# A feed-forward made from the residual times the norm's weight, with the norm's inverse by token multiplied into gate and value

## What is computed

```python
def rms_norm_2(x, gain):
    xf = x.astype(jnp.float32)
    y = xf * lax.rsqrt(jnp.mean(xf * xf, axis=-1, keepdims=True) + EPS)
    return (y * gain.astype(jnp.float32)).astype(x.dtype)
...
        mix = jnp.concatenate([lru_o, gla_o], axis=-1) @ w_out[l]
        x = x + mix

        h = rms_norm_2(x, norm2[l])
        gate, up = jnp.split(h @ w_ffn_in[l], 2, axis=-1)
        x = x + (jax.nn.silu(gate) * up) @ w_ffn_out[l]
    return rms_norm_2(x, final_norm)
```

## Time and profile before

| | us |
|---|---|
| median of 3 timed runs | 2332.33 (2331.25 to 2334.07) |
| profiled execution, its time | 2328.58 |
| profiled execution, its span | 2327.3 |
| TensorE busy in the span | 2258.5 (97%) |
| VectorE busy | 1410.2 (61%) |
| ScalarE busy | 1045.0 (45%) |
| GpSimd busy | 985.5 (42%) |

### The profile page before, as it was taken

One profiled execution on the slowest core, in us unless ns is written; L12 is line 12 of the kernel. 1 busy time (PEld: TensorE's weight loads), 2 busy tenths in 40 slices (PEclk: granted clock), 3 DMA queues, 4 the chain that ended last, 5 costly groups with the idle time before them and its releaser, 6 DMA issues.

```text
span 2327.3 us, 29639 instructions
## 1 busy us (share of the span) xinstructions
PE 2258.5 (97%) x11342; PEld 1795.0 (77%) x11342; DVE 1410.2 (61%) x1784; ACT 1045.0 (45%) x1644; POOL 985.5 (42%) x674
## 2 busy tenths in 40 slices
PE   5999999999999999999999999999999999999998
PEld 5888755478888888866688677888878888888887
DVE  6256678668885275268845663442876666666665
ACT  5323265488883264357734562222333333333334
POOL 1111188546652138853122121122365555665551
PEclk9999999999999999999999999999999999999999
DMA  8255300010003133220031311132111111111111
GB/s 318 78 154 161 118 1 5 5 34 1 1 1 118 37 130 109 73 73 11 34 103 43 126 37 37 37 118 64 28 54 55 55 55 55 54 46 47 55 55 73
DMA packets 156385, 154.74 MB, mean 66 GB/s; under 512 B 12550, under 2 KB 141620, under 8 KB 154324
## 3 DMA queue, kind: packets, MB, share of 16 engines
q1 hardware_dynamic: 156244, 152.84, 21.1%
HBM read 128.05 MB, written 20.97 MB: 64 GB/s over the span
## 4 chain that ended last, share of the span: by engine, by line
PE 84%; ACT 5%; DVE 4%; issue 3%; POOL 2%; DMA 1%; SPq 0%; ACTq 0%; DVEq 0%; POOLq 0%
PE ps L256 29%; PE ps L3219 15%; PE ps L3236 9%; PE ps L1946 6%; PE ps L1366 3%; PE ps L1377 2%; PE ps L1165 2%; PE ps L2256 2%; PE ps L2239 2%; PE ps L2225 2%; PE ps L1188 2%; PE ps L1175 1%; PE ps L1348 1%; POOL WSL L3136 1%; ACT B_PR L1249 1%
## 5 line engine op out<-in xcount | busy, mean ns | idle before, releaser
L243 POOL TENSOR_TENSOR WL<-WR,WH 128x1024 fp32r<-128x1024 f32 (+2 forms) x71 | 163.9, 2309 | 656.2 <-ACT WH L238 656.0
L256 PE MATMUL ps<-HH,WH 128*128 128x512 f32 (+2 forms) x880 | 279.8, 399 | 0.4 <-issue 0.3
L256 PE MATMUL ps<-HL,WH 128*128 128x512 f32 (+2 forms) x880 | 273.6, 392 | 0.0
L256 PE MATMUL ps<-HH,WL 128*128 128x512 f32 x848 | 263.2, 392 | 0.0
L3449 DVE TENSOR_TENSOR XF<-ps,XF 128x1024 f32<-128x1024 f32 x168 | 201.6, 1220 | 32.5 <-PE ps L3236 25.9
L3219 PE MATMUL ps<-HC,WSH 128*128 128x512 f32 x640 | 197.1, 389 | 0.0
L256 PEld LDWEIGHTS ps<-HL,WH 128*128 128x128 f32 (+2 forms) x880 | 164.0, 186 | 37.7
L256 PEld LDWEIGHTS ps<-HH,WH 128*128 128x128 f32 (+2 forms) x880 | 160.2, 187 | 38.1 <-issue 5.3
L256 PEld LDWEIGHTS ps<-HH,WL 128*128 128x128 f32 x848 | 160.5, 189 | 34.2
L3136 POOL TENSOR_TENSOR WSL<-WSR,WSH 128x512 fp32r<-128x512 f32 x100 | 131.4, 1314 | 107.5 <-ACT WSH L3130 107.5
L3130 ACT ACTIVATE WSH<-WSR 128x512 fp32r<-128x512 f32 x100 | 62.9, 629 | 218.2 <-POOL WSR L3118 218.2
(11 more groups left out here) (460 smaller groups left out, 5309.6 us busy)
## 6 DMA issues: line engine op xcount, KB each, us to landing
WS<-in_w_ffn_in SPq DMA_DIRECT2D x44, 512.0 KB, 5.1
MKW<-in_ada_w SPq DMA_DIRECT2D x32, 512.0 KB, 4.1
spill<-X SPq DMA_DIRECT2D x3, 4096.0 KB, 13.9
OW<-in_w_ffn_out SPq DMA_DIRECT2D x22, 512.0 KB, 3.6
WR<-in_w_in SPq DMA_DIRECT2D x19, 512.0 KB, 3.8
WR<-in_even_w_in SPq DMA_DIRECT2D x17, 512.0 KB, 4.1
AWK<-in_ada_w SPq DMA_DIRECT2D x8, 1024.0 KB, 9.3
X<-spill SPq DMA_DIRECT2D x2, 4096.0 KB, 13.6
```

Source lines behind the costliest of these rows:

```text
L243: pool.tensor_tensor(low[:, :, :], raw[:, :, :], high[:, :, :].bitcast(F32), ALU.subtract).then_inc(*w_low.up(t))
L256: last = pe.matmul(ps[0:w.out, 2 * s + h, :], wt[:, k, :], x[:, k, halves(h)], start=(k == 0 and n == 0), stop=(k == w.kt - 1 and n == len ...
```

## The change

- The blocks are made from the residual times `norm2` alone, without the inverse by token. So they no longer wait for the norm: each follows its output tile on VectorE, its high part is made by ScalarE and its low part by VectorE. HC is laid out anew, by feature, so that a block may overwrite those parts of HM and LM that the last output tile has read.
- The token sums and the spread are made between the products of pair 0, whose order is by pairs of features (0, 4), (1, 5), (2, 6), (3, 7). The `pe_stay_awake` around them goes.
- ScalarE copies the spread inverse to TOKENS. Gate and value are multiplied by it: in pairs 0 and 1 as they leave PSUM (`dve_plain`, 1024 wide), in pairs 2 to 21 by four instructions of 512 on VectorE (`dve_by_token`). Silu then reads CG.
- TOKENS takes the place at 139.5 KB, where OWL was; OWL now lies on OW (131.5 KB). So OW(j) may be loaded only after y(j-1, 7), the last that reads the parts before it. The last pair has an OW of its own. SP asks for WS a pair earlier in its list.
- In pair 1 the tiles of y(0) stand otherwise between the products: 2, 3, 3 and none.

```diff
     def pe_second_out():
         for f, t in enumerate(S_OUT):
-            pe_tile(t, HM, LM, made=(lambda k: m_low.at(2, k)) if f == 0 else None)
-        pe_stay_awake(8, 4)
-        pe_token_sums(3, 4, LAST.sq)
-        pe_stay_awake(5, 5)
-        pe_spread(3, LAST)
-        pe_stay_awake(13, 0)
+            if f < DT - 1:
+                pe_tile(t, HM, LM, made=(lambda k: m_low.at(2, k)) if f == 0 else None)
+        for k in range(DT):
+            last = pe_feature(t, k, HM, LM)
+            if k % 2 and k < DT - 1:
+                last.then_inc(*out_freed.up("mix", k))
...
             dve_residual(t, f, at=LAST)
+            dve_block(f)
             dve_add_square(3, f, LAST.sq)
+        for k in BLOCKS[:4]:
+            dve_block_low(k)
         dve_last_residual(t, at=LAST)
+        dve_block(DT - 1)
+        for k in BLOCKS[4:6]:
+            dve_block_low(k)
         for h in range(2):
             dve_add_last_square(3, h, LAST.sq)
+        for k in BLOCKS[6:]:
+            dve_block_low(k)
...
-    OW = place("OW", 131.5, [P, DM])
+    OW = [place("OW0", 131.5, [P, DM]), place("OW1", 63, [P, DM])]
     A_OW = [[place(f"{n}{i}", kb, [P, SEQ], F32R) for n, kb in zip(("AH", "AL", "OWH", "OWL"), kbs)]
-            for i, kbs in enumerate(((115, 127.5, 135.5, 139.5), (51, 55, 59, 63)))]
+            for i, kbs in enumerate(((115, 127.5, 135.5, 131.5), (39, 47, 55, 63)))]
+    TOKENS = place("TOKENS", 139.5, [P, SEQ])
...
         for j in range(NPAIR):
             if j:
-                sp_pair(j)
+                if j + 1 < NPAIR:
+                    sp_pair(j + 1)
+                sp.wait_ge(*(y_done.at(j - 1, DT - 1) if j < NPAIR - 1 else ws_used.at(at_use(j, M5))))
                 sp.wait_ge(*ow_low.at(j - 1))
             else:
                 sp.wait_ge(*w_used.at(S_OUT[-1]))
-            sp.dma_start(OW[:, :], d["w_ffn_out_2"][0][rows(j), :]).then_inc(*ow_loaded.landed(j))
+            sp.dma_start(out_weight(j), d["w_ffn_out_2"][0][rows(j), :]).then_inc(*ow_loaded.landed(j))
+            if j == 0:
+                sp_pair(1)
...
         else:
             dve.wait_ge(*b_low.at("block", DT - 1))
-            if o != M3:
-                dve.wait_ge(*b_sum.at(M3, 1))
+            dve.wait_ge(*(spread_turned.at(3) if o == M3 else b_sum.at(M3, 1)))
...
         if o == M5:
             dve_add(j, "3+5", M5, CG[:, N2], CG[:, N2], bank[BANK[M5]], copied=(M5, 0))
+            dve_by_token(j, CG, "gate", 1, "3+5")
...
             dve_add(j, "value", M1, CU[:, N2], CU[:, N2], bank[BANK[M1]], waits=("3-2+6",))
+            dve_by_token(j, CU, "value", 0, "2+4")
+            dve_by_token(j, CU, "value", 1, "value")
             dve_product(j, 1)
         elif o == M7:
             dve_add(j, "gate", M7, CG[:, N1], CG[:, N1], bank[BANK[M7]], waits=("1+4-5",))
+            dve_by_token(j, CG, "gate", 0, "gate")
             dve_a_low(j, 1)
             dve_product(j, 0)
             dve_a_low(j, 0)
 
+    def dve_by_token(j, values, name, h, made):
+
+        dve.wait_ge(*m_added.at(j, made))
+        dve.tensor_tensor(values[:, halves(h)], values[:, halves(h)], TOKENS[:, halves(h)], ALU.mult).then_inc(
+            *m_added.up(j, "scaled " + name, h))
+
+    def dve_plain(j, g, name, values):
+
+        if g == 0 and j == 0:
+            dve.wait_ge(*scale_copied.at("tokens"))
+        elif g == 0:
+            dve.wait_ge(*product_made.at(j - 1, 1))
+        dve.wait_ge(*ws_used.at(at_use(j, 2 * g + 1)))
+        dve.tensor_tensor(values[:, :], pair(2 * g), TOKENS[:, :], ALU.mult).then_inc(*m_added.up(j, name))
```

More of the change, by code:

```diff
@@ L2999, in more @@
                     act_weight_high(0, o)
+                for k in BLOCKS[:-1]:
+                    act_block_high(k)
         act_out_tiles(S_OUT, 3, more, at=LAST)
+        act_block_high(BLOCKS[-1])
         act_root(3)
@@ L3190, in pe_plain @@
             pe.wait_ge(*b_low.at("block", k))
-        elif k == 0:
-            pe.wait_ge(*(product_made.at(j - 1, 1) if g else silu_made.at(j - 1)))
+        if k == 0:
+            pe.wait_ge(*(m_added.at(j - 1, "value" if g else "gate") if j else ev_dve.at(S_OUT[DT - 2:][(S_OUT[0] + g) % 2])))
         for m, (w, x) in enumerate(((WSH, 0), (WSH, 1), (WSL, 0))):
             for n in range(2):
-                last = pe.matmul(ps[:, 2 * g + n, :], w[:, q % RING, i, :], HC[c][:, n, x, i, :], start=(k == 0 and m == 0),
+                last = pe.matmul(ps[:, 2 * g + n, :], w[:, q % RING, i, :], HC[c][:, i, n, x, :], start=(k == 0 and m == 0),
                                  stop=(k == DT - 1 and m == 2))
@@ L3211, in pe_product @@
         elif j == NPLAIN:
-            pe.wait_ge(*(silu_made.at(j - 1) if o in (M3, M5) else product_made.at(j - 1, 1)))
+            pe.wait_ge(*m_added.at(j - 1, "gate" if o in (M3, M5) else "value"))
         else:
@@ L3304, in act_out_high, with act_inverse_by_token @@
             act.wait_ge(*y_done.at(j - 1, DT - 1))
-        act.activation(buffers(j)[2][:, :], OW[:, :], ACT.Copy).then_inc(*ow_high.up(j))
+        act.activation(buffers(j)[2][:, :], out_weight(j), ACT.Copy).then_inc(*ow_high.up(j))
+    def act_inverse_by_token():
+        act.wait_ge(*spread_turned.at(3))
+        act.activation(TOKENS[:, :], pair(6), ACT.Copy).then_inc(*scale_copied.up("tokens"))
     def act_silu(j):
-        act.wait_ge(*ws_used.at(at_use(j, 1)))
-        if j:
-            act.wait_ge(*product_made.at(j - 1, 1))
-        act.activation(CG[:, :], pair(0), ACT.Silu).then_inc(*silu_made.up(j))
+        act.wait_ge(*m_added.at(j, "gate"))
+        act.activation(CG[:, :], CG[:, :], ACT.Silu).then_inc(*silu_made.up(j))
     def act_silu_half(j, h):
-        act.wait_ge(*m_added.at(j, "3+5" if h else "gate"))
+        act.wait_ge(*m_added.at(j, "scaled gate", h))
         act.activation(CG[:, halves(h)], CG[:, halves(h)], ACT.Silu).then_inc(*silu_made.up(j, h))
     def act_ffn():
-        for f in range(DT):
-            act_block_high(f)
-            if f in (3, 4):
-                act_weight_high(1, f - 3)
+        act_weight_high(1, 0)
+        act_weight_high(1, 1)
+        act_inverse_by_token()
         act_out_high(0)
+        act_operand_high(M3)
         act_silu(0)
@@ L3325, in act_ffn @@
         act_weight_high(1, 3)
-        act_operand_high(M3)
         act_a_high(0, 0)
@@ L3451, in dve_ffn @@
     def dve_ffn():
-        dve.wait_ge(*spread_turned.at(3))
-        for f in range(DT + 1):
-            if f < DT:
-                dve_block(f)
-            if f:
-                dve_block_low(f - 1)
         dve_operand_sum(M3)
@@ L3469, in dve_ffn @@
                         dve_operand_low(M6)
+            dve_plain(j, 0, "gate", CG)
+            dve_plain(j, 1, "value", CU)
             dve_product(j, 0)
```

47 lines of the change are left out of this document (27 added, 20 removed).

## The result

The changed kernel takes 2427.33 us (median of 4 runs, 2420.74 to 2428.79), the kernel before 2331.79 on the same chip (2327.08 to 2334.07). The ratio is 1.0406, 95% interval 1.0393 to 1.0419: 95.5 us slower, where 85 were forecast. The profiled execution has a span of 2425.2 us, 97.9 more than before.

The account below looks back on a forecast made before the run. TensorE was taken to bound the kernel, so a change saves only holes or makes new ones. Boundary -2.6, pairs +84.6 and tail +2.9 sum to +85 on 2332.3, giving 2417 us; range 2355 to 2435.

Parts of the forecast that it names:

- The steady pair: Pairs 2 to 19: late OW, port clashes and multiplications delay a, then y(2); +4.7 us a pair, +84.6 in all.
- The boundary: Hole before the feed-forward up to pair 2: hole closed, 5.4 us wait before pair 1; -3.0, then -2.6 us.
- Pair 3: Already waits 2.0 us at the steady pair's place; moves by about as much, since VectorE comes to it later.
- The tail: Last pair and end: M4 waits for a copy, +1.7 us; y(21,0) waits for a, +1.2; together +2.9.
- The clock: TensorE's granted clock, which stayed at 1.00 after a comparable idle stretch, was taken to stay up despite two waits a pair.
- rival 3: Steady pairs: the clock falls too, 0.85 over 11 us of each pair; 30 us more, 2447 us; chance 0.09.
- Rival 1: Steady pairs: OWL out of the way, only multiplications cost, 1.4 us a pair; sum +25, 2358 us; chance 0.17.

Follow-up runs that it names:

- the new order: Changed kernel with all its work kept but ScalarE, VectorE and GpSimd taking it in another order in pairs 2 to 21: 2351.54 us, ratio 1.0096 to the kernel before.
- the start alone: Changed kernel with OW loaded early again and no multiplications by token in pairs 2 to 21: 2330.92 us, ratio 0.9996 to the kernel before.
- the kernel with OW early: Changed kernel with OWL in its own place, OW loaded half a pair earlier, multiplications kept: 2408.38 us, ratio 1.0326 to the kernel before.

## Why the prediction was right, and where it was off

**The steady pair: right.** Place by place: OWH at T+1.10 (1.15 forecast), product 1 ended at 5.49 (5.55), a's second half at 10.17 (10.38), y(0) at 10.32 (10.5), y(2) at 18.15 (18.3), period at full clock 34.60 (34.6). The three steps behind it were each shown: late OW and the multiplications by leaving one out at a time; the port by moving OWL, for product 0 in the new order (2.11 to 0.69); the way from a to y(2) by moving the copies. Of the 97.9 us of the profiled execution 9.7 are falls and 4.6 the offset; the 83.6 that are left are close to the sum's 84.9. So the steady pair's price was no luck; the 10 us by which 85 was short of the measured 95.5 are about what the falls cost.

**The boundary: mis-sized.** "-3.0, and after one more y(2) like today's, with a multiplication in front, -2.6" came out as -2.3 at pair 2's first product (1692.32, less the offset of 4.6), -1.0 at y(1,0) and -0.6 at y(1,2). The wait for gate's multiplication was foreseen and is 5.04 where 5.4 was said. Pair 1 starts 1.3 us earlier than forecast (1657.46, less the offset, against 1654.1). What the sum lacked is behind that: the fall at pair 1's start takes 1.7, y(1,0) waits 1.18 for a where it waited for nothing before, and y(1,2)'s wait grew to 3.12 from 2.86. The experiment with the start alone puts the whole of it between -0.14% and +0.05%.

**Pair 3: right in sum, with its wait in another place.** y(2,0) waits 3.84 us, not the 1.99 of the steady pairs, and y(2,2) only 0.49. In the kernel before the two waits are 0.21 and 1.40, 1.6 in all where "2.0" was said. From y(1,2) to y(3,0) the changed kernel takes 7.9 us more, 1.6 of it the fall; that leaves 6.2 where 7.0 was said (2.3 and 4.7). So the +5.0 of the table's third line is in part made good in the fourth. The rows show why this y(2,0) waits longer. In pair 2 VectorE still makes M7's sum and low part. It begins the additions behind M1 at T+2.60 instead of T+0.20 (T is 1726.27), and a's second half ends at T+12.02, 1.85 later than in a steady pair:

```profile
1721.65 3.83 DVE L3201 TENSOR_TENSOR HS<-RAW,HS 128x1024 fp32r<-128x1024 f32 x2
...
1728.87 0.67 DVE L3434 TENSOR_TENSOR CG<-CG,ps 128x512 f32<-128x512 f32 x1
```

**The tail: right.** The forecast was +1.7 and +1.2; the waits are 1.33, and 1.41 where it was 0.21, which makes +1.6 and +1.2. The rest of the table's excess there is the fall behind y(19,2).

**The clock: wrong as a condition.** "After a comparable idle stretch (7.14 busy of 10) the granted clock stayed at 1.00" was the argument for giving rival 3 only 9 in 100. It came in with a part of its 30 us: six falls that cost, 9.7 us. One stretch of the kernel before at 1.00 said nothing of waits that come back in every pair. The granted clock went to half (0.50, so 1.2 GHz) behind waits of 2.0 and 2.1 us in some pairs and not in others, and with filler in the waits in none from y(3,0) on. The Trainium skill, "TensorE: Matmul & The Clock Gate", section "HAM oscillation — how this bites in real kernels", tells of a kernel whose matmuls were back at the slow clock at every wait. The runs agree with it here for some of the waits only, 9 of 34.

**Not in the forecast at all:** 4.6 us ahead of the change's first instruction. In the thirteen traces of this case the residual of tile 0, up to which the kernels do the same, comes between 1546.5 and 1553.3 us, so a single trace has that much of its own, and the median's 95.5 is the better figure than the span's 97.9.

**Rival 1** ("only the multiplications stay", 25 us) would have been too small even if OW had come early: the experiment shows +3.1 a pair, where 1.4 was said. Product 1 ends at T+5.17 and a at T+8.56, not at 3.5 and about 7.1, since with OWL out of the way the multiplications and product 1 still run beside GpSimd's next pieces (2.08 for two multiplications, 1.59 for the product).

## What to carry to other kernels

Lay one steady period out with every engine's deadline before the work in it is added to: VectorE was idle for 39% of the span before, but had 0.3 us of room at one addition, and 2.8 us of multiplications and a load that came 3.6 us later cost 4.7 us in each steady pair. Where a step must be added there, try other places in the list: the same instructions in another order took 1.0% more than the kernel before instead of 4.1%. A start made earlier is worth only what the next engine's list lets through, and moving a single instruction to the front may only move the wait.

## What the hardware showed that was not expected

- Waits of TensorE of 2.0 and 2.1 us that come back every 34.6 us were followed in nine of 34 places from y(3,0) on by 8 to 10 matmuls at half pace, which take 1.6 us more than at full pace. In the kernel with OW early there were 11 falls in 16 pairs behind waits of 2.1, with waits of only 0.39 at y(0); without the multiplications, two in 17 behind waits of 1.6 to 2.0. Which wait is followed by a fall could not be told from the rows.
- A wait's figure is less than what it costs: with waits of 4.09 us the period grew by 4.66. Of the 0.57 between, 0.32 is how the figure is counted: it starts at the end of the matmul before, 0.39 after that one's start, where the next would have started after 0.23. The other 0.24 is lost behind the waits, where the first rows start 0.54 to 0.56 apart instead of 0.45.
- VectorE's 128x512 product of two SBUF operands took 0.69 us alone and 2.11 and 2.69 beside GpSimd's 128x1024 difference, which itself took 2.70 to 2.85 instead of 2.40. By the Trainium skill, "SBUF — State Buffer", section "Who interferes with whom", such instructions block each other for their whole length. The trace agrees, since the product's excess of 1.4 and 2.0 us is not more than what was left of GpSimd's instruction.
